# Two attention items at every place between matmul passes, with a fourth probability buffer

## The reference, cut to what matters

```python
proj = jnp.einsum('bsd,de->bse', h, w_in) + b_in
# A: sparse attention, 8 heads; an indexer picks the 128 best keys of each token
score = jnp.einsum('bqhs,bqh->bqs', jax.nn.relu(logits), iwb)
_, sel = lax.top_k(score, n_sel)
p = jax.nn.softmax(s, axis=-1); o = jnp.einsum('bhgqn,bqnhd->bqhgd', p, v_sel)
# B: chunked attention, 8 heads, with a learned relative-position bias
s = jnp.einsum('bqhd,bkhd->bhqk', qb, kb) * scale + bias[None]
p = jax.nn.softmax(s, axis=-1); o = jnp.einsum('bhqk,bkhd->bqhd', p, vb)
# C: mLSTM, 4 heads; q and k pass a depthwise convolution of 4 taps and SiLU first,
#    the decay comes from a running sum of log_sigmoid(f_pre)
qk = jax.nn.silu(causal_depthwise_conv(jnp.concatenate([c_q, c_k], axis=-1), conv_w, conv_b))
s_qk = jnp.einsum('bhcld,bhcsd->bhcls', qc, kc) * jnp.exp(D - m_row[..., None])
merged = jnp.sum(gate * y, axis=2)
return x + jnp.einsum('bsd,de->bse', merged, w_out)
```

## Time and profile before

| | |
|---|---|
| median of three runs | 1332.26 us |
| profiled execution | 1330.72 us, span 1328.9 us |
| granted TensorE clock over the span | 0.996 |
| PE busy | 1287.5 us, 97% |
| DVE, ACT, POOL busy | 54%, 47%, 46% |
| chain that ended last | PE 81%, DVE 10%, ACT 4%, issue 3% |
| passes of the units with h (L591) | 3 x 1136, 392 to 400 ns each in the profile |

### The profile page before, as it was taken

How to read it: one execution, slowest core, us unless ns; L and a number is a source line. 1 busy time by engine, 2 the same in 40 slices (tenths; PEclk the granted TensorE clock), 3 DMA queues, 4 the chain that set the end, 5 groups by cost and what they waited for, 6 DMA issues and landing times.

```text
span 1328.9 us, 19950 instructions
## 1 busy us (share of the span) xinstructions
PE 1287.5 (97%) x6525; PEld 1080.2 (81%) x6525; DVE 714.4 (54%) x1444; ACT 621.8 (47%) x1119; POOL 610.0 (46%) x767
## 2 busy tenths in 40 slices
PE   5999999999999999999999999999999999999997
PEld 3788888888987888887878888888888878888876
DVE  5678888856347112112657897977544532121155
ACT  4444666776444323333344456577754333323332
POOL 3556333342224555545765543334321545455472
PEclk9999999999999999999999999999999999999998
DMA  5322211222132233333142221112213222322321
GB/s 182 144 89 93 95 49 51 77 73 71 34 127 65 83 100 101 95 101 104 66 175 94 96 96 64 48 58 86 64 49 111 80 80 87 103 95 87 103 95 63
DMA packets 37030, 117.39 MB, mean 88 GB/s; under 512 B 4064, under 2 KB 6496, under 8 KB 36448
## 3 DMA queue, kind: packets, MB, share of 16 engines
q1 hardware_dynamic: 34368, 111.37, 25.2%
q10 hardware_dynamic: 2592, 5.11, 1.2%
HBM read 110.18 MB, written 6.29 MB: 88 GB/s over the span
## 4 chain that ended last, share of the span: by engine, by line
PE 81%; DVE 10%; ACT 4%; issue 3%; POOL 1%; DMA 0%; ACTq 0%; DVEq 0%; SPq 0%; POOLq 0%
PE acc L591 65%; PE ps_o L704 4%; PE ps_t L691 3%; DVE score L1179 1%; PE ps_t L682 1%; PE ps_o L711 1%; PE ps_s L661 1%; DVE top L1178 1%; PE ps_s L667 1%; DVE att_c L1311 1%; POOL w_lo L540 1%; DVE ak_s L1152 1%; PE spare L643 1%; ACT prob L937 1%; PE ps_s L675 1%
## 5 line engine op out<-in xcount | busy, mean ns | idle before, releaser
L540 POOL TENSOR_TENSOR w_lo<-w_raw,w_hi 128x256 fp32r<-128x256 f32 x752 | 598.7, 825 | 687.2 <-ACT w_hi L786 687.2
L591 PE MATMUL acc<-h_hi,w_hi 128*128 128x512 f32 x1136 | 454.2, 400 | 0.3 <-ACT w_hi L786 0.3
L591 PE MATMUL acc<-h_lo,w_hi 128*128 128x512 f32 x1136 | 445.4, 392 | 0.0
L591 PE MATMUL acc<-h_hi,w_lo 128*128 128x512 f32 x1136 | 297.1, 395 | 2.1 <-POOL w_lo L540 2.1
L786 ACT ACTIVATE w_hi<-w_raw 128x1024 fp32r<-128x1024 f32 (+1 forms) x212 | 203.9, 962 | 130.8 <-PE acc L591 100.6
L591 PEld LDWEIGHTS acc<-h_hi,w_hi 128*128 128x128 f32 x1136 | 213.8, 188 | 40.8 <-ACT w_hi L786 0.7
L591 PEld LDWEIGHTS acc<-h_lo,w_hi 128*128 128x128 f32 x1136 | 213.8, 188 | 39.6
L591 PEld LDWEIGHTS acc<-h_hi,w_lo 128*128 128x128 f32 x1136 | 208.2, 188 | 43.2 <-POOL w_lo L540 2.9
L1324 DVE SCALAR_TENSOR_TENSOR gated<-prob,acc 128x512 f32<-128x512 f32 x16 | 11.0, 688 | 247.6 <-PE acc L591 247.6
L987 ACT ACTIVATE prob<-acc,par_half 128x512 f32<-128x512 f32 x48 | 33.0, 688 | 148.4 <-PE acc L591 148.4
L937 ACT ACTIVATE prob<-prob,neg_max 128x128 f32<-128x128 f32 (+3 forms) x128 | 70.6, 552 | 19.5 <-DVE neg_max L1214 19.0
(11 more groups left out here) (239 smaller groups left out, 1819.9 us busy)
## 6 DMA issues: line engine op xcount, KB each, us to landing
w_raw<-w_full SPq DMA_DIRECT2D x164, 512.0 KB, 3.4
w_raw<-w_mix SPq DMA_DIRECT2D x48, 256.0 KB, 2.6
x_kept<-xT SPq DMA_DIRECT2D x2, 2048.0 KB, 9.1
rel<-rel ACTq DMA_DIRECT2D x16, 256.0 KB, 2.7
xT<-x_kept SPq DMA_DIRECT2D x2, 2048.0 KB, 9.2
stage<-x SPq DMA_DIRECT2D x4, 512.0 KB, 7.0
out<-stage SPq DMA_DIRECT2D x4, 512.0 KB, 3.0
consts<-consts ACTq DMA_DIRECT2D x1, 640.0 KB, 4.1
```

The lines of the kernel that those rows point to most:

```text
L540: last = pool.tensor_tensor(w_lo[:, slot, part, :], w_raw[:, raw, part, :], w_hi[:, slot, part, :].bitcast(F32), ALU.subtract)
L591: last = pe.matmul(acc[slot][:, :], w[:, slot, k, :], x[:, k, :], start=(i == 0), stop=(i == 3 * nk - 1))
```

## The change

`push` now takes a pair of items: both scores, both exps at the same place, then turn_p of the pair before and values of the pair before that (for branch C the pair's own turn_p, and values of the pair before). So there are half as many places for items, 74 places per layer instead of 116, and one or two per unit stand where three stood, two where four stood, between runs of passes twice as long. exp moves one place forward in ACT's stream: ahead of the unit that ends next. `prob` has a fourth buffer, whose room comes from `ones`, now 128 wide; the scans read its first column broadcast.

```diff
--- before.py
+++ after.py
@@ -30,6 +30,7 @@
 DC = D // P
 HEADS, HD = 8, 64
 IDX_HEADS = 4
+PROBS = 4
 TOPK = 128
 CH = 4
 BR = 4
@@ -82,21 +83,22 @@
     seq = []
     flying = []
 
-    def push(n):
+    def push(*items):
 
 
         seq.append(CUT)
-        if n is not None:
-            seq.append(("scores", n))
-        flying.append(n)
-        mlstm = any(m is not None and m >= 64 for m in flying[-4:])
-        for back, kind in ((1, "exp"), (2, "turn_p"), (3, "values")) if mlstm else ((2, "exp"), (3, "turn_p"), (4, "values")):
-            if len(flying) >= back and flying[-back] is not None:
-                seq.append((kind, flying[-back]))
+        seq.extend(("scores", n) for n in items)
+        flying.append(items)
+        seq.extend(("exp", n) for n in items)
+        lag = 0 if any(n >= 64 for new in flying[-2:] for n in new) else 1
+        for back, kind in ((lag, "turn_p"), (lag + 1, "values")):
+            if len(flying) > back:
+                seq.extend((kind, n) for n in flying[-1 - back])
 
     def flush():
-        for _ in range(3):
-            push(None)
+        push()
+        if not any(n >= 64 for new in flying for n in new):
+            push()
         flying.clear()
 
     def units(a, b):
@@ -150,22 +152,24 @@
     for u in range(first, 38):
 
         units(u, u + 1)
-        upto = -(-64 * (u + 1 - first) // (38 - first))
+        upto = 2 * -(-32 * (u + 1 - first) // (38 - first))
         k = 0
         while n < upto:
-            push(n)
-            if work:
-                seq.append(work.pop(0))
-            seq.extend(STACK_AT.get(n, []))
-            if n == 31:
-                rows = 0
-            if n >= 32 and n % NT == NT - 1 and (n - 32) // NT + 2 < HEADS:
-                seq.append(("rel_bias", (n - 32) // NT + 2))
+            push(n, n + 1)
+            for n in (n, n + 1):
+                if work:
+                    seq.append(work.pop(0))
+                seq.extend(STACK_AT.get(n, []))
+                if n == 31:
+                    rows = 0
+                if n >= 32 and n % NT == NT - 1 and (n - 32) // NT + 2 < HEADS:
+                    seq.append(("rel_bias", (n - 32) // NT + 2))
             n += 1
             if k == 0:
                 seq.extend(soon)
                 soon = []
-            if k == 1:
+            k += 1
+            if n >= upto:
                 seq.extend(late)
                 late = []
                 if rows == 6:
@@ -173,7 +177,6 @@
                     rows += 1
                 if u == U_AZ + 1:
                     seq.append(("turn_c", 0))
-            k += 1
         if 0 <= rows < 6:
             seq.append(("rows", rows))
             rows += 1
@@ -191,9 +194,9 @@
     assert n == 64
     for u in range(38, 42):
         units(u, u + 1)
-        for k in range(NT):
-            push(n)
-            n += 1
+        for k in range(0, NT, 2):
+            push(n, n + 1)
+            n += 2
             if k == 2:
                 seq.extend(late)
                 late = []
@@ -380,7 +383,7 @@
         assert 1280 * 4 + ROW <= 1152 * 4 + 2 * ROW
 
         consts = sb("consts", [P, KCOLS])
-        ones = sb("ones", [P, SEQ])
+        ones = sb("ones", [P, P])
         ident_b = sb("ident_b", [P, P], BF16)
         causal_b = sb("causal_b", [P, P], BF16)
         par_next = sb("par_next", [P, PCOLS])
@@ -388,7 +391,7 @@
         par_half = sb("par_half", [P, PCOLS])
         par_eighth = sb("par_eighth", [P, PCOLS])
         gains = sb("gains", [P, (DEPTH + 1) * DC])
-        prob = sb("prob", [P, 3, SEQ])
+        prob = sb("prob", [P, PROBS, SEQ])
         prob_t = sb("prob_t", [P, 2, SEQ])
         turn = sb("turn", [P, SEQ])
         norm = sb("norm", [P, SEQ])
@@ -688,7 +691,7 @@
                             pe.wait_ge(turn_free[n % 2], l * (ITEMS // 2) + n // 2 + FREE)
                             pe.wait_ge(prob_ready, l * ITEMS + n + 1)
                             for s in range(t + 1):
-                                last = pe.transpose(ps_t[n % 2][:, s * P:(s + 1) * P], prob[:, n % 3, s * P:(s + 1) * P], ident)
+                                last = pe.transpose(ps_t[n % 2][:, s * P:(s + 1) * P], prob[:, n % PROBS, s * P:(s + 1) * P], ident)
                             last.then_inc(turn_full, 1)
                     elif kind == "values":
                         branch, h, t = item(n)
@@ -934,20 +937,20 @@
                         branch, h, t = item(n)
                         if branch != "c":
                             act.wait_ge(max_ready, l * 64 + n + 1)
-                            act.activation(prob[:, n % 3, 0:(t + 1) * P], prob[:, n % 3, 0:(t + 1) * P], ACT.Exp,
+                            act.activation(prob[:, n % PROBS, 0:(t + 1) * P], prob[:, n % PROBS, 0:(t + 1) * P], ACT.Exp,
                                            bias=neg_max[:, n % 4:n % 4 + 1], scale=-1.0,
                                            accum_out=row_sum[:, n % 8:n % 8 + 1]).then_inc(prob_ready, 1)
                         else:
                             use = SCORE_USE[("scores", n)]
                             act.wait_ge(score_full, l * SCORE_USES + use + 1)
-                            if n < 67:
-                                act.wait_ge(turn_full, l * ITEMS + n - 2)
+                            if n < 64 + PROBS:
+                                act.wait_ge(turn_full, l * ITEMS + n - PROBS + 1)
                             else:
-                                act.wait_ge(turn_free[(n - 3) % 2], l * (ITEMS // 2) + (n - 3) // 2 + 1 + FREE)
+                                act.wait_ge(turn_free[(n - PROBS) % 2], l * (ITEMS // 2) + (n - PROBS) // 2 + 1 + FREE)
                             if n == 64:
                                 act.wait_ge(spare_free, l * SPARE_USES + SPARE_USE[("turn_c", 0)] + 3 + FREE)
                             for s in range(t + 1):
-                                last = act.activation(prob[:, n % 3, s * P:(s + 1) * P], ps_s[use % 2][:, s * P:(s + 1) * P],
+                                last = act.activation(prob[:, n % PROBS, s * P:(s + 1) * P], ps_s[use % 2][:, s * P:(s + 1) * P],
                                                       ACT.Exp, bias=source_t[:, s, h:h + 1])
                             last.then_inc(prob_ready, 1)
                             act.wait_ge(prob_ready, l * ITEMS + n + 1)
...
@@ -1273,7 +1276,7 @@
                         s = n - 2
                         w = SEQ - s * P
 
-                        link(dve.tensor_tensor_scan(decay[:, SUM_AT[s]:SUM_AT[s] + w], ones[0:CH, 0:w], f_row[:, s * P:SEQ], 0.0,
+                        link(dve.tensor_tensor_scan(decay[:, SUM_AT[s]:SUM_AT[s] + w], ones[0:CH, 0:1].broadcast_to([CH, w]), f_row[:, s * P:SEQ], 0.0,
                                                     ALU.mult, ALU.add))
                         link(dve.tensor_tensor(source[:, s * P:(s + 1) * P], i_row[:, s * P:(s + 1) * P],
                                                decay[:, SUM_AT[s]:SUM_AT[s] + P], ALU.subtract))
```

More of the change, by code:

```diff
@@ L1223, in _ @@
                             w = (t + 1) * P
-                            dve.scalar_tensor_tensor(prob_t[:, n % 2, 0:w], ps_t[n % 2][:, 0:w], 0.25 * P ** -0.5, prob[:, n % 3, 0:w],
+                            dve.scalar_tensor_tensor(prob_t[:, n % 2, 0:w], ps_t[n % 2][:, 0:w], 0.25 * P ** -0.5, prob[:, n % PROBS, 0:w],
                                                      ALU.mult, ALU.mult).then_inc(turn_free[n % 2], 1)
```

2 lines of the change are left out of this document (1 added, 1 removed).

## The result

The changed kernel takes 1363.89 us (median, 1363.74 to 1364.21), the kernel before 1332.12 in the same comparison: ratio 1.0242, 95% interval 1.0224 to 1.026. The forecast was 1340.5, range 1325 to 1350. The span grew by 33.5 us, about half of it in each layer: the last products of branch C's gates (`z_c` 3) start at 444.69 us in layer 1, before at 427.66 (17.0 later), and at 1103.23 in layer 2, before at 1070.50 (15.7 more); 0.8 us come behind that.

What follows compares the result with a forecast made beforehand. PE, busy 97% of 1328.9 us, was taken as the bound. Waits, 2 x (12.8 - 7.0) = +11.6, and fewer places, -3.4, took 1330.72 to 1338.9; with the median 1.5 higher, 1340.5 us, range 1325 to 1350.

Steps and rivals of the forecast that it cites:

- term 1: Fewer switches on PE: 84 places fewer in both layers at 0.04 us each, -3.4 us (0 to -5.0).
- term 3: New PE waits as ACT and DVE take turns; with the start's 1.5, waits after are 12.8 us per layer.
- Item 36: PE waits at its scores for head 1's `bk_lo`: 5.3 us per layer (3.7 to 7.4).
- The chain of head 1: DVE and ACT steps up to head 1's `bk_lo`, ending at E + 21.2; PE is there at E + 16.9.
- E: End of the place of items (30, 31), from which head 1's steps are counted in us.
- Item 42: PE waits for the bank that a DVE maximum frees: 3.5 us per layer (3.1 to 4.1).
- Start: PE waits because DVE comes late out of topk: 1.6 us per layer before, 1.5 after.
- items 48 and 60: PE waits for `bk_lo` of heads 4 and 7: 0.4 and 0.8 us per layer.
- units 25 to 27: Copies of transposes stand behind two exps; PE waits for a free `ps_t`: 1.0 us per layer (0 to 2.7).
- Term 2: Old waits in the attention stretch, 7.0 us per layer, all go except the start's.
- much slower: Rival: DVE late from unit 23 on, head 1 costs 7.4, units 25 to 27 2.7; 1350 to 1356 us; chance 0.10.
- Absorbed: Rival: DVE and ACT keep ahead; only start and heads 4 and 7 wait, 2.7 us per layer; 1320 us; chance 0.22.

Runs made afterwards that it cites:

- Run 2: Changed kernel with dummy passes on PE (28, 15 and 8) ahead of item 36's scores, item 42's scores and `z_a` 1: 1355.37 us, ratio 1.0189.
- 3: Kernel before, single items and three buffers, with exps moved to their item's own place: 1355.64 us, ratio 1.0179.
- 8: Changed kernel with each pair's exps on ACT moved to the end of the pair's place: 1354.39 us, ratio 1.017.
- 10: Changed kernel with ACT's rounded halves of the stacked queries and keys (`bq_hi`, `bk_hi`) a pair early: 1349.16 us, ratio 1.0127.
- 12: Changed kernel with ACT's rounded halves a pair early and each pair's exps at the end of its place: 1345.66 us, ratio 1.0103.
- 16: Changed kernel with ACT's halves early, exps last, the convolution's second half first and `bk_lo` early: 1337.09 us, ratio 1.0038.
- 15: Kernel before, single items, with the gate and a unit's other late steps moved beside the convolution's second half: 1341.08 us, ratio 1.0068.
- 13: Kernel before, single items, with four probability buffers and transposes and values of branches A and B one place later: 1336.95 us, ratio 1.0037.

## Why the prediction was wrong

The direction was right, and so was the place of the two largest waits and what they are for; the size wasn't: +33.5 us of span against +8.2. Of the 25.3 us between them, some 15.8 are the price of the waits, 6.6 their own length and 2.9 term 1. By its own steps:

- **The step that failed: the price of a wait in term 3.** It took a wait as the idle time and no more. In the profile TensorE's clock falls to half in or behind the three longest, and the work behind them then takes 2.24 + 4.05 + 1.64 = 7.9 us per layer longer, 15.8 in all. Run 2 bounds what of it is lost time: 8.5 us come back when nothing but idleness is taken away. It also shows that the clock isn't all: with it at 1.00 the time is 1355.4 us, still above the range, so waits sized too small fail beside it. The prediction forecast waits of 5.3 and 3.5 us where the kernel before has none over 1.7 in its attention stretches, and nowhere looked at what a long one does. The trace of before has two outside them: PE idle for 2.78 us until 29.40 and for 2.50 until 1315.53. The windows of before around them:

```profile
28.00:32.00 4.00, 2.58 (x14) 2.26 (x15) 2.51 (x4) 1.29 (x2) 2.98 (x3) 0.95 0.28 97
32.00:36.00 4.00, 4.00 (x11) 2.79 (x11) 0.92 (x3) 2.45 (x6) 0.00 (x0) 0.62 1.05 349
36.00:40.00 4.00, 4.00 (x19) 3.24 (x18) 2.79 (x4) 1.91 (x4) 3.92 (x5) 1.00 0.72 307
...
1316.00:1320.00 4.00, 2.19 (x11) 2.14 (x11) 1.40 (x5) 1.43 (x3) 0.00 (x0) 0.50 0.00 0
```

  The 0.62 and the 0.50 there were the warning.
- **Term 3's waits themselves**: 16.1 us in layer 1 against 12.8. Item 36: 6.85, forecast 5.3 (3.7 to 7.4). The chain of head 1 went as summed, from `norm` on. E is 223.65; `norm` ends at 228.27, E + 4.6, where the sum has E + 2.1, and `bk_lo` ends at 247.45, E + 23.8, where it has E + 21.2. What it had at nothing is, for the most part, the gate's wait of 1.91 us for its tanh (226.86 in DVE's rows above): the tanh stands on ACT behind two exps, which wait for DVE's maxima. The 1 us added for a late DVE was too little. Item 42: 3.78 and 3.4, forecast 3.5 (3.1 to 4.1). Start 1.3 (1.5), items 48 and 60 0.38 and 1.47 (0.4 and 0.8), item 40 none (0.3), units 25 to 27 0.3 (1.0). Not in the list at all: `z_a` 1, 2.0 us. The places were found by following one engine's queue at a time; this one hangs on a bank that `turn_c` frees, a step the prediction did not list as moved.
- **Term 2**: right. The exp waits are gone, and what all waits of before cost was 7.3 us per layer, forecast 7.0.
- **Term 1**: -3.4 is not borne out. From the first item to the last `z_c` the layers take 16.6 and 15.8 us longer, 32.4 together. Waits and slow work come to 16.1 + 7.9 - 7.3 = 16.7 in layer 1 and, with layer 2's own waits (15.9, before 7.6), to 16.2 there. So about -0.5 us is left for all 84 places, good to half a microsecond or so. In branch C, from item 62 to the last `z_c` of layer 1, the kernel before takes 101.22 us and the changed one 101.25; the changed one has 11 places fewer there but 2 passes and 6 products of values more (1.1 us), and before has 0.9 us of waits: again some 0.02 us per place. What the prediction worked out from the Trainium skill's figure for a weight load (TensorE: Matmul & The Clock Gate, LDWEIGHTS), that pairing saves nothing, was nearer than the 0.04 per place read as a remainder of rounding. (the earlier trace rows are of item 37's place, 256 keys, and not of item 38's; the sum is the same.)
- **The bounds**: the low and high ends named in term 3 add to 9.5 and 17.8 us per layer, not 9.1 and 18.7, so 1332 to 1354; the measured time is above either.
- **The rival "much slower"** (1350 to 1356) had DVE's lateness ahead of head 1 right, its cause too (the gates wait for the tanh), but not the 2.7 us at units 25 to 27 (0.3), and it has the same flaw in its price. "Absorbed" rested on half-idle engines; 3 and 8 show that idle time on ACT counts for nothing when it stands in front of an instruction that others queue behind.

What made the waits is shown by runs 8, 10, 12 and 16, which undo it in the paired order without undoing the pairs: with ACT's halves of the keys early, exps last, the convolution first and `bk_lo` early, 26.8 of the 31.8 us are gone, and with eight dummy passes 30.2. So pairing by itself brings nothing and costs next to nothing (1.0003 to 1.0021 times the kernel before in the mended order with dummy passes, 1.0024 to 1.0052 without them). What it takes away is the place that lay between a step on one engine and its answer on the other: runs 3 and 15 put two such round trips into the old order and cost 24 and 9.5 us there. Their sum, 33.6, is close to the loss of the change, 31.8; that it is so by more than chance isn't shown, and in 3 PE waits for copies at the values, not for keys. Open are also why the logarithm costs 8.7 us more in either other place of the mended order (only the waits were read), and 13.

## What to carry to other kernels

Price a long wait on TensorE as its idle time and the slow work behind it, here 1.6 to 4.1 us, less what that work would have had to wait for anyway; look in the trace at hand for waits of that length and the granted clock behind them, in more than one place, since the same wait isn't always followed by a fall. When steps are merged into fewer places, look in each engine's queue for pairs "A waits for B, and B's answer is queued behind something that waits for A": spread them over two places, and keep an instruction that waits for a far engine last in its place. Issuing a blocked instruction earlier makes it no earlier and everything behind it late.
